# A convolution module in fp32 split form: a group's banded matmuls placed between the products of the following group

## What is computed

```
a, bgl, g = jnp.split(h @ w_in, 3, axis=-1)
u = a * jax.nn.sigmoid(bgl)
u = lax.conv_general_dilated(u, w_dw, window_strides=(1,), padding=[(CONV_PAD, CONV_PAD)],
                             dimension_numbers=('NWC', 'WIO', 'NWC'),
                             feature_group_count=CONV_W) + b_dw
u = jax.nn.silu(layer_norm(u, g_ln, b_ln)) * jax.nn.silu(g)
return u @ w_o
```

## Time and profile before

| | us |
|---|---|
| median of 3 runs (3260.82 to 3264.07) | 3262.49 |
| the profiled execution, time | 3262.19 |
| its span, first to last instruction | 3260.2 |
| first product of `conv_in` starts, from the span's start | 2294.99 |
| `conv_out`'s first loads are issued | 2994.90 |

### The profile page before, as it was taken

How to read it: one execution, slowest core, us unless ns; L and a number is a source line. 1 busy time by engine, 2 the same in 40 slices (tenths; PEclk the granted TensorE clock), 3 DMA queues, 4 the chain that set the end, 5 groups by cost and what they waited for, 6 DMA issues and landing times. The chain is left out here.

```text
span 3260.2 us, 44295 instructions
## 1 busy us (share of the span) xinstructions
PE 3001.7 (92%) x15091; PEld 2495.0 (77%) x15091; DVE 1757.5 (54%) x2927; ACT 1422.4 (44%) x2971; POOL 431.0 (13%) x285
## 2 busy tenths in 40 slices
PE   2999999699999999999999998996899999997798
PEld 2878878588888878787878886784688888886677
DVE  6654554366766666767676765435233323333554
ACT  3554545356555655555555554325111111112543
POOL 1000000010111111110111110003011111112331
PEclk9999999899999999999999999997899999998899
DMA  6546455511112121211111100533222222213443
GB/s 219 182 158 228 147 178 182 174 51 44 51 33 69 40 70 40 69 36 44 50 55 54 40 27 29 203 127 123 71 70 70 65 68 73 70 54 125 134 155 103
DMA packets 217944, 308.07 MB, mean 94 GB/s; under 512 B 81008, under 2 KB 142720, under 8 KB 216576
## 3 DMA queue, kind: packets, MB, share of 16 engines
q1 hardware_dynamic: 213120, 296.98, 28.0%
q10 hardware_dynamic: 4608, 8.39, 0.7%
HBM read 213.94 MB, written 91.37 MB: 94 GB/s over the span
## 5 line engine op out<-in xcount | busy, mean ns | idle before, releaser
L1086 ACT ACTIVATE at_prob<-at_S,at_nmax 128x512 f32<-128x512 f32 (+1 forms) x640 | 411.4, 659 | 371.6 <-DVE at_nmax L1200 367.8
L1223 DVE TENSOR_TENSOR at_ptlo<-at_T,at_pthi 128x512 fp32r<-128x512 f32 x576 | 396.7, 689 | 319.4 <-ACT at_pthi L1102 318.3
L1102 ACT ACTIVATE at_pthi<-at_T 128x512 fp32r<-128x512 f32 x576 | 349.2, 609 | 225.4 <-PE at_T L972 225.4
L1189 DVE TENSOR_REDUCE at_mx<-at_S 128x1 f32<-128x512 f32 (+1 forms) x640 | 393.6, 630 | 84.2 <-PE at_S L946 77.4
L972 PE MATMUL at_T<-ident,at_prob 128*128 128x128 f32 x2304 | 345.8, 272 | 3.2 <-DVE at_ptlo L1223 3.2
L972 PEld LDWEIGHTS at_T<-ident,at_prob 128*128 128x128 f32 x2304 | 278.3, 140 | 69.4 <-DVE at_ptlo L1223 16.6
L95 PE MATMUL ci_ps<-h1hi,ci_whi 128*128 128x512 f32 x768 | 300.1, 391 | 17.6 <-DVE ci_wlo L1651 17.6
L96 PE MATMUL ci_ps<-h1lo,ci_whi 128*128 128x512 f32 x768 | 299.8, 390 | 0.0
L97 PE MATMUL ci_ps<-h1hi,ci_wlo 128*128 128x512 f32 x768 | 299.7, 390 | 0.0
L941 PE MATMUL at_S<-at_khi,at_qhi 128*128 128x512 f32 (+1 forms) x640 | 249.7, 390 | 48.6 <-ACT at_prob L1086 25.8
L95 PE MATMUL at_O<-at_pthi,at_vhi 128*128 128x512 f32 x576 | 272.8, 474 | 0.6 <-DVE at_og L1232 0.5
(11 more groups left out here) (202 smaller groups left out, 6391.9 us busy)
## 6 DMA issues: line engine op xcount, KB each, us to landing
fr_w<-in_w_front SPq DMA_DIRECT2D x75, 512.0 KB, 4.1
at_wmod<-in_w_mod SPq DMA_DIRECT2D x32, 512.0 KB, 3.3
ci_w<-in_cv_w_in SPq DMA_DIRECT2D x24, 512.0 KB, 4.2
fr_w<-in_w_front SPq DMA_DIRECT2D x24, 384.0 KB, 3.9
values<-fr_ob SPq DMA_DIRECT2D x36, 256.0 KB, 2.9
at_kst<-k_nope SPq DMA_DIRECT2D x8, 1152.0 KB, 7.3
at_vst<-values SPq DMA_DIRECT2D x8, 1152.0 KB, 7.3
fr_x<-in_x SPq DMA_DIRECT2D x16, 512.0 KB, 6.6
```

The lines of the kernel that those rows point to most:

```text
L1086: nc.scalar.activation(prob[:, j % 2, i, k], S[:, c, 0:k.stop - k.start], ACT.Exp, scale=SCALE, bias=nmax[:, i % 2:i % 2 + 1], accum_out=l ...
L1102: nc.scalar.activation(dst, T[:, (n + SLOTS * j) % 2], ACT.Copy).then_inc(s_hi, 1)
L1189: nc.vector.tensor_reduce(mx[:, i % 2, c:c + 1], S[:, c, 0:k.stop - k.start], AXX, ALU.max).then_inc(s_mx, 1)
L1223: nc.vector.tensor_tensor(ptlo[:, kt % 3], T[:, (n + SLOTS * j) % 2], pthi[:, kt % 3].bitcast(F32), ALU.subtract).then_inc(s_lo, 1)
```

## The change

TensorE's order is changed, and that of the other engines with it. The chunks of a group no longer follow its gates in one run. Chunk n of group g - 1 follows product n of group g. The last group has no following group; its own chunks stand between its own gates, in the order `TAIL`. Group 1 is written out beside group 0 and group 7, since its predecessor is the first group, and the loop runs over groups 2 to 6.

On SP, the reloads of `raw`, the stores of z, the weight loads and the stores of `u` are placed step by step beside the products. On ScalarE and VectorE each step prepares chunk n + 1 and finishes chunk n - 1. GpSimd's order is unchanged; its wait for the constants stands before its first group as before, and ScalarE's and VectorE's wait for the constants moves to the front of group 0. Loop bounds, buffers and the operations themselves stay as they are. The core of the diff:

```diff
+        TAIL = ("G0", "G1", 0, 1, 2, "G2", 3, 4, 5, "G3", 6, 7)
+
         def loop(eng, body):
             body(0, True, False)
-            with eng.Fori(1, GROUPS - 1) as g:
+            body(1, False, False)
+            with eng.Fori(2, GROUPS - 1) as g:
                 body(g, False, False)
             body(GROUPS - 1, False, True)
...
 # SP
+                for n in range(CH):
+                    if not first:
+                        reload_u(g - 1, n)
+                        if n:
+                            store_z(g - 1, n - 1)
+                    if not last and n < 3:
+                        sp.wait_ge(s_wlo, g * 3 + (n + 1))
+                        load_w(sp, g + 1, n)
+                    if n % 2:
+                        store_u(g, n // 2)
                 if not first:
-                    sp.wait_ge(s_ulo, g * CH)
+                    store_z(g - 1, CH - 1)
                 for k in range(2):
                     sp.wait_ge(s_ust[k], g * 32 + 32)
                 for q in range(4):
                     load_u(sp, g, q)
+                if not last:
+                    for b in range(NBLK):
+                        store_gate(g, b)
+                else:
+                    for x in TAIL:
+                        if isinstance(x, int):
+                            reload_u(g, x)
+                            store_z(g, x)
+                        else:
+                            store_gate(g, int(x[1]))
...
 # ScalarE
+                    u_high(g - 1, 0)
+                for n in range(CH):
+                    if not first:
+                        if n:
+                            evict_z(g - 1, n - 1)
+                        if n + 1 < CH:
+                            u_high(g - 1, n + 1)
+                    if n % 2 == 0:
+                        act.wait_ge(s_ab, g * 8 + (n + 1))
+                        sigmoid(g, n // 2, ps[:, n % 6], first)
+                    if n == 0:
                         w_high(act, g, G, first)
+                if not first:
+                    evict_z(g - 1, CH - 1)
...
 # VectorE
+                    band_and_low(g - 1, 0)
+                for n in range(CH):
+                    if not first and n + 1 < CH:
+                        band_and_low(g - 1, n + 1)
+                    b = n // 2
+                    if n % 2:
+                        dve.wait_ge(s_ab, g * 8 + (n + 1))
+                        product(g, b, ub[:, b % 2], ps[:, n % 6],
+                                None if first and b < 2 else (s_ust[b % 2], g * 32 + 16 * (b // 2)))
+                    if n == 1:
                         w_low(g, G)
...
 # TensorE
                         product(g, s, n % 6, b).then_inc(s_ab, 1)
+                        if not first:
+                            convolve(g - 1, n)
                 pe.wait_ge(s_wlo, g * 3 + 3)
+                if not last:
+                    for b in range(NBLK):
+                        gate(g, b)
+                else:
+                    for x in TAIL:
+                        if isinstance(x, int):
+                            convolve(g, x)
+                        else:
+                            gate(g, int(x[1]))
```

More of the change, by code:

```diff
@@ L1607, in sigmoid, with u_high, evict_z, gate @@
                 nc.scalar.activation(sig[:, n % 2], src, ACT.Sigmoid).then_inc(s_sig, 1)
-            def body(g, first, last):
[L1610 to L1613, removed]
+            def u_high(g, q):
+                act.wait_ge(s_raw[q % 4], g * 32 + 16 * (q // 4 + 1))
+                if not isinstance(g, int) or g or q >= 2:
+                    act.wait_ge(s_cv, g * CH + (q - 1))
+                nc.scalar.activation(uhi[:, q % 2, HALO:HALO + NCOL], raw[:, q % 4], ACT.Copy).then_inc(s_uhi, 1)
+            def evict_z(g, q):
+                act.wait_ge(s_cv, g * CH + (q + 1))
+                if not isinstance(g, int) or g or q >= 2:
+                    act.wait_ge(s_zst[q % 2], g * 64 + 16 * (q // 2))
+                nc.scalar.activation(zb[:, q % 2], ps[:, 6 + q % 2, 0:NCOL], ACT.Identity,
+                                     bias=bdw[:, bass.ds(g * CH + q, 1)]).then_inc(s_z, 1)
+            def gate(g, b):
+                act.wait_ge(s_g, g * 4 + (b + 1))
+                sigmoid(g, NBLK + b, ps[:, (8 + b) % 6], False)
+            def body(g, first, last):
+                if first:
+                    act.wait_ge(s_const, 32)
+                    act.wait_ge(s_pad, 1)
+                else:
[10 more added lines that the diff above has]
+                    if n == 0:
                         w_high(act, g, G, first)
+                if not first:
+                    evict_z(g - 1, CH - 1)
                 if not last:
@@ L1621, in body @@
                 nc.scalar.activation(thi[:], taps[:], ACT.Copy).then_inc(s_thi, 1)
[L1622 to L1640, removed]
+                if not last:
+                    for b in range(NBLK):
+                        gate(g, b)
+                else:
+                    gate(g, 0)
+                    u_high(g, 0)
+                    u_high(g, 1)
+                    for x in TAIL[1:]:
+                        if isinstance(x, int):
+                            evict_z(g, x)
+                            if x + 2 < CH:
+                                u_high(g, x + 2)
+                        else:
+                            gate(g, int(x[1]))
             loop(act, body)
@@ L1660, in product, with band_and_low, gate @@
                                         ALU.mult).then_inc(s_mul, 1)
-            def body(g, first, last):
[L1663 to L1667, removed]
+            def band_and_low(g, q):
+                if not isinstance(g, int) or g or q >= 2:
+                    dve.wait_ge(s_cv, g * CH + (q - 1))
+                nc.vector.tensor_tensor(bhi[:, q % 2], *banded(thi[:, q].bitcast(F32)), ALU.mult).then_inc(s_bhi, 1)
+                dve.wait_ge(s_uhi, g * CH + (q + 1))
+                nc.vector.tensor_tensor(ulo[:, q % 2, HALO:HALO + NCOL], raw[:, q % 4],
+                                        uhi[:, q % 2, HALO:HALO + NCOL].bitcast(F32), ALU.subtract).then_inc(s_ulo, 1)
+            def gate(g, b):
+                product(g, NBLK + b, gb[:, b % 2], ps[:, (8 + b) % 6],
+                        None if isinstance(g, int) and g == 0 and b < 2 else (s_gst[b % 2], g * 32 + 16 * (b // 2)))
+            def body(g, first, last):
+                if first:
+                    dve.wait_ge(s_const, 32)
+                else:
+                    band_and_low(g - 1, 0)
[8 more added lines that the diff above has]
+                    if n == 1:
                         w_low(g, G)
@@ L1675, in body @@
                 nc.vector.tensor_tensor(tlo[:], taps[:], thi[:].bitcast(F32), ALU.subtract).then_inc(s_tlo, 1)
[L1676 to L1688, removed]
+                if not last:
+                    for b in range(NBLK):
+                        gate(g, b)
+                else:
+                    gate(g, 0)
+                    band_and_low(g, 0)
+                    band_and_low(g, 1)
+                    for x in TAIL[1:]:
+                        if isinstance(x, int):
+                            if x + 2 < CH:
+                                band_and_low(g, x + 2)
+                        else:
+                            gate(g, int(x[1]))
             for s in (B, A):
@@ L1701, in product, with convolve, gate @@
                 return mm
+            def convolve(g, q):
+                pe.wait_ge(s_ulo, g * CH + (q + 1))
+                pe.wait_ge(s_bhi, g * CH + (q + 1))
+                pe.wait_ge(s_blo, g * CH + (q + 1))
+                if not isinstance(g, int) or g or q >= 2:
+                    pe.wait_ge(s_z, g * CH + (q - 1))
+                for j in range(OFFS):
+                    w = [t[:, q % 2, j].rearrange("p c f -> p (c f)") for t in (bhi, blo)]
+                    mm = split3(nc, ps[:, 6 + q % 2, 0:NCOL], w[0], w[1], uhi[:, q % 2, j:j + NCOL],
+                                ulo[:, q % 2, j:j + NCOL], j == 0, j == OFFS - 1)
+                mm.then_inc(s_cv, 1)
+            def gate(g, b):
+                n = 8 + b
+                if n % 2 == 0:
+                    pe.wait_ge(s_sig, g * 8 + ((n - 6) // 2 + 1))
+                else:
+                    pe.wait_ge(s_mul, g * 8 + ((n - 6) // 2 + 1))
+                product(g, G, n % 6, b).then_inc(s_g, 1)
             def body(g, first, last):
@@ L1744, in _, with bands @@
         def _(pool):
-            def body(g, first, last):
-                if first:
-                    pool.wait_ge(s_const, 32)
+            def bands(g):
                 pool.wait_ge(s_tlo, g + 1)
                 for q in range(CH):
-                    if not first or q >= 2:
+                    if not isinstance(g, int) or g or q >= 2:
                         pool.wait_ge(s_cv, g * CH + (q - 1))
                     nc.gpsimd.tensor_tensor(blo[:, q % 2], *banded(tlo[:, q]), ALU.mult).then_inc(s_blo, 1)
```

(5 more changed lines are left out.)

31 lines of the change are left out of this document (14 added, 17 removed).

## The result

| | us |
|---|---|
| kernel before, median of 4 runs (3260.82 to 3264.07) | 3261.79 |
| changed kernel, median of 4 runs (3211.01 to 3217.26) | 3214.39 |
| ratio | 0.985, 95% interval 0.9836 to 0.9864 |
| span of the profiled execution | 3213.2 |

The forecast was 3208, in 3202 to 3222. On two other chips the changed kernel gave 3209.42 (ratio 0.9843, 0.9829 to 0.9856) and 3212.88 (0.9851, 0.9838 to 0.9865) in five runs each, where the kernel before gave 3261.4 and 3260.88. So the gain is 47 to 52 us, 1.5%.

The account below looks back on a forecast made before the run. TensorE, busy 92% of the span, bounds the kernel, with holes in the banded runs. Holes and chunks fall from 171.6 to 117.2 us (114.6 + 1.1 + 1.5), gaining 54.4: 3208 us, range 3202 to 3222.

Parts of the forecast that it names:

- Price of a chunk, 1.79 us: Banded matmuls on TensorE: a chunk of 15 matmuls that follows running work costs 1.79 us, 64 of them 114.6.
- Cover of product 0, 2.4 us to spare: Groups 0 to 6: a 5.44 us product covers chunk 0's preparation of 3.06 us, leaving 2.4 to spare.
- SP's queue, the loads into raw, the stores of z, the weights: nothing: DMAs on SP's in-order queue: reloads, weight loads and stores now alternate, land before they are wanted and cost nothing.
- The switch between the two forms, 1.1 us in all, bounds 0 to 0.41 each: TensorE switching between 512 and 256 columns: 0.02 us for each of 57 returns to a product, 1.1 in all.
- The last group's two gaps of 0.73: Last group: chunks 2 and 5 each start after a gap of 0.73 us, 1.5 us together.
- The stage, 642: From TensorE's first product to the last banded matmul's start: 642 us where it took 696.6.
- Behind the stage, zero, plus or minus 3 us for the clock's phase: The convolution's output stage: no change, with 3 us kept on both sides for when its work meets the clock's return.
- Work neither comes nor goes: Whole change: same matmuls, same VectorE, ScalarE, GpSimd and DMA instructions; only their order moves.
- The time, 3208: Whole kernel: 3208 us after a gain of 54.4; with everything hidden 3203 to 3214, chance 0.80.
- the tax: Rival: chunks behind products still cost 2.20 us, so 26 us of gain stay away: 3234, half 3221; chance 0.12.
- the overlap is there: Rival of no overlap: a wait holds the product instead, holes move there, time stays at 3262; chance 0.03.
- the clock did not fall: Rival: chunks between products begin at 1.2 GHz, 1.46 us more each, 82 us for 56: 3290; chance 0.05.

Follow-up runs that it names:

- before_again: The kernel before once more, unaltered, for a second trace: 3265.48 us in one run.
- twice_before: The kernel before with VectorE's high bands made twice for every chunk, the first copy unread: 3312.13 us, ratio 1.0159.
- pad_before: The kernel before with 48 small unused matmuls on TensorE at the stage's start, meant to move the instruction fetch: 3265.49 us, ratio 1.0019.
- pad_after: The changed kernel with 40 small unused matmuls on TensorE at the stage's start, to move the instruction fetch: 3212.03 us, ratio 0.9857.
- peel2: The changed kernel with group 2 written out as well, the loop over groups 3 to 6: 3213.67 us, ratio 0.9848.
- again: The changed kernel once more, unaltered, for a second trace: 3209.42 us, ratio 0.9843.
- control: The changed kernel once more, unaltered, third trace, on the same chip beside the version with group 2 written out: 3212.88 us, ratio 0.9851.
- split_only: The kernel before with group 1 written out ahead of the loop and no order changed: 3262.95 us, ratio 1.0006.
- one_run: The changed kernel with a group's eight chunks in one run behind product 0 of the following group: 3231.25 us, ratio 0.9915.
- twice_after: The changed kernel with VectorE's high bands made twice for every chunk, the first copy unread: 3214.35 us, ratio 0.986.

## Why the prediction was right, point by point

The stage went by the mechanism that was forecast. The terms outside it did not. Twelve traces, grouped by where the fetch falls, tell the parts apart:

| trace | fetch from the last matmul, us | first use of z from there | behind the stage |
|---|---|---|---|
| before, before_again, twice_before | none in -10 to +40 | 8.6, 8.7, 8.6 | 268.6, 268.6, 269.6 |
| pad_before, pad_after, peel2 | -1.1, -8.5, -6.6 | 9.0, 8.7, 8.6 | 267.8, 267.5, 270.0 |
| changed, again, control | 4.4, 4.4, 5.0 | 11.1, 10.1, 10.0 | 272.1, 270.7, 271.2 |
| split_only, one_run, twice_after | 4.5, 4.3, 4.4 | 10.2, 10.0, 10.4 | 272.2, 271.6, 270.5 |

- *Price of a chunk, 1.79 us.* Right: 1.78 and 1.79.
- *Cover of product 0, 2.4 us to spare.* Right: 2.46 in the group shown. With the high bands made twice it still held, with 1.7 to spare.
- *SP's queue, the loads into raw, the stores of z, the weights: nothing.* Right; behind its start the stage has no wait of TensorE on any of them.
- *The switch between the two forms, 1.1 us in all, bounds 0 to 0.41 each.* Right in kind, half the size: 0.011 each, 0.6 us for 58 returns to a product (the prediction counts 57).
- *The last group's two gaps of 0.73.* Right to 0.01 each: 2.51 - 1.79 = 0.72 both times. The sum leaves out that the stage's last matmul lasts 0.16 longer than its step.
- *The stage, 642.* Measured 642.0, 641.0 and 642.1: a gain of 54.6 to 55.6 where 54.4 was the sum. The 1 us between them is the first product, which takes 8.36, 7.36 and 8.48; behind it all three have 633.6, where the kernel before has 688.3, a gain of 54.7.
- *Behind the stage, zero, plus or minus 3 us for the clock's phase.* This failed. The first trace has 3.5 us more there, over the 3 that the prediction itself names as a sign of being wrong; the other two have 2.1 and 2.6. The six traces with a fetch among the opening loads have 270.5 to 272.2, the six without 267.5 to 270.0, on the mean 271.4 and 268.7. Of these 2.7 us, 1.6 lie ahead of the first use of z, where the two kinds of traces do not overlap (10.0 to 11.1 against 8.6 to 9.0), and where neither order nor clock but the fetch tells them apart. The other 1.1 lie behind it, where they do overlap (260.1 to 262.0 against 258.8 to 261.4); their cause stays open. The step that failed is the sentence "Work neither comes nor goes", which looked at instructions that are executed and not at the program's text: group 1 is written out. The diff shows that by itself, and I did not ask what it does.
- *The time, 3208.* The first measurement, 3214.39, lies 0.4 us outside the range that the prediction gives for its own mechanism (3203 to 3214). It is in the range as a whole because that was widened for the tax, which did not come: that much is luck. The remaining 4 us of the first trace lie ahead of the stage, for which the prediction has no term; there the start scatters over 2294.8 to 2298.9 in four traces of kernels in the old order and over 2297.0 to 2300.5 in six in the new one, the ones with small matmuls left out. The means differ by 1.5 us, which so few traces can't tell from nothing; whether the longer text costs something there too stays open.

The rivals: the tax is refuted by the rows, the overlap is there, and once it had risen in the first product the clock did not fall until the stage's end. What the prediction says for the tax, that every chunk start in the banded runs but one shows a gap, was misread: chunk 1 shows none in rows 5 either, nor in any of the eight banded runs of that trace. The rule of the Trainium skill, page "TensorE: Matmul & The Clock Gate", section "A second HAM failure mode: psum-queue depth-cycling", that I had set against the change did not apply: two sets of banks in turn left no standstill between products and chunks in the middle group, and the granted clock was 1.00. The other rule, of 262 cycles for 256 columns, was again not met by this form: the step is 0.119 us and not 0.109.

## What to carry to other kernels

A stage in which one engine bounds can still hold short runs bounded by another engine's chain; look for them stretch by stretch, and see whether the run can be cut up among work that the chain can hide behind before you try to make the chain shorter. What a piece will cost then can be read off a place in the old trace where its inputs happened to be ready, here the one chunk start of rows 6. Count the program's text as part of a change: an iteration written out moves instruction fetches, and here one that fell among the loads on which a stage opens went with 1.0 to 2.4 us that no reordered instruction explains.

## What the runs showed of the hardware that I had not expected

A fetch of 16 KB of program text among the output stage's opening loads goes with a slower opening. One of SP's issues takes longer: the two for the gate 2.05 to 3.65 us instead of 1.05 in five traces, the one behind them 1.74 instead of 0.82 in the sixth, the control. The second load of z lands 9.9 to 11.0 us behind the last matmul instead of 8.5 to 8.9. Fetch and late landing go together in twelve traces, whether the fetch was brought in (the text alone made longer) or moved out; by what way 16 KB do it, no run shows.

VectorE and GpSimd in each other's way: with GpSimd idle the high bands took 0.82 and the low half 0.42 us. In the kernel before and in the change 48 of GpSimd's 64 operations met VectorE's bands and low halves, and 48 of these grew, by 0.8 to 1.1 us: one for each. GpSimd's own took 1.29 alone and mostly 1.93 beside them. VectorE's gate products, with one input from PSUM, did not grow (1.08 to 1.11 beside GpSimd). Once, in the kernel before with doubled bands:

```profile
2557.85 0.83 DVE L1685 TENSOR_TENSOR ci_extra<-ci_thi,ci_mask 128x640 f32<-128x640 f32 x1 [0.99 <-PE ci_ps L97]
2558.59 1.91 DVE L1686 TENSOR_TENSOR ci_bhi<-ci_thi,ci_mask 128x640 fp32r<-128x640 f32 x1
2560.43 0.41 DVE L1688 TENSOR_TENSOR ci_ulo<-ci_raw,ci_uhi 128x256 fp32r<-128x256 f32 x1
...
2557.90 1.93 POOL L1754 TENSOR_TENSOR ci_blo<-ci_tlo,ci_mask 128x640 fp32r<-128x640 f32 x1 [21.50 <-PE ci_ps L97]
```

The three take turns: VectorE's first one ends at 2558.68, GpSimd's at 2559.83, and VectorE's second at 2560.50, 0.67 behind it and 1.91 long for 0.82. In rows 7 it was the low half that was long (1.28). The Trainium skill, page "SBUF — State Buffer", section "Who interferes with whom", says that a VectorE instruction with two inputs from SBUF contends with a GpSimd instruction that reads SBUF, because its second input comes through an interface that the two share; the trace agrees, with 0.8 to 1.1 us a time.
